# One written order with filling for the stages ahead of the experts, and inverse roots on VectorE

## The reference, cut to what matters

```python
mod = (s_c @ ada_w[l] + ada_b[l])            # 6 x 1024 columns: shift, scale, gate, twice
hx = rms_norm(x, norm1_g[l]) * (1.0 + sc1) + sh1
px = hx @ w_in                               # 2304 columns, split into groups A, B, C, D
ya = chunk_spatial_gating(aX, sgu_w, sgu_b)  # gelu, heads of v normed, a 128 x 128 product a head
yb = fourier_mix(bX)                         # two products with DFT matrices
yc = diff_attn_core(...)                     # group C: two softmaxes a head, their difference times v
yd = neighbourhood_attn_latent(...)          # group D: one softmax a head, with a window and a bias
y_lat = rms_norm(heads of [ya, yb, yc, yd], head_g) @ w_out
x = x + g1 * y_lat
aff = softmax((rms_norm(x, norm2_g[l]) * (1.0 + sc2) + sh2) @ router_w)   # 16 experts
gate, idx = top_k(aff.T, 32)                 # each expert takes 32 of 256 tokens
x = x + g2 * scatter(silu(xg @ wg) * (xg @ wu) @ wd * gate)
```

## Time and profile before

| | |
|---|---|
| median of 3 runs | 3203.36 us (3201.06 to 3207.66) |
| profiled execution | 3201.78 us, of it span 3200.0 us |
| TensorE / VectorE / ScalarE busy | 2916.9 / 908.9 / 550.2 us |
| mean granted TensorE clock | 0.946 |
| HBM read | 667 MB, 209 GB/s over the span |

### The profile page before, as it was taken

The page is one execution under the profiler, slowest core; times in us unless marked ns, Lnnn a source line. Parts: engine busy times, 40 slices in busy tenths (PEclk is TensorE's granted clock), DMA queues, the critical chain, the costliest instruction groups (busy, mean ns, idle before and its releaser), DMA issues.

```text
span 3200.0 us, 32009 instructions
## 1 busy us (share of the span) xinstructions
PE 2916.9 (91%) x12620; PEld 1682.0 (53%) x12620; DVE 908.9 (28%) x1838; ACT 550.2 (17%) x1059; POOL 91.3 (3%) x159
## 2 busy tenths in 40 slices
PE   6997689888889987999898999999999999999998
PEld 3554334333335544333333585665784686674883
DVE  2545431111114453101111343452100434343001
ACT  1243311111111241110110113230000113310000
POOL 3000000000001000000000100001000000000000
PEclk9997689999999987998988999999999999999999
DMA  9313129999996333999999542224434432224432
GB/s 283 127 49 125 53 88 410 410 410 410 410 405 198 119 138 132 374 409 410 410 410 407 169 154 71 92 74 139 157 116 167 151 131 79 85 74 161 154 130 81
DMA packets 237359, 669.76 MB, mean 209 GB/s; under 512 B 8064, under 2 KB 18616, under 8 KB 237248
## 3 DMA queue, kind: packets, MB, share of 16 engines
q1 hardware_dynamic: 230432, 653.28, 54.2%
q0 software_dynamic: 6816, 14.94, 2.0%
HBM read 667.09 MB, written 2.90 MB: 209 GB/s over the span
## 4 chain that ended last, share of the span: by engine, by line
PE 75%; DMA 17%; DVE 4%; issue 2%; ACT 1%; POOL 0%; SPq 0%; DVEq 0%; ACTq 0%; POOLq 0%
PE bank L768 31%; DMA ring<-in_exp_w_up_dram 16%; PE bank L781 9%; PE bank L1302 9%; PE bank L1320 5%; PE bank L1154 4%; PE bank L981 3%; PE bank L302 3%; PE bank L1177 1%; PE bank L921 1%; PE bank L1116 1%; PE bank L1032 1%; PE bank L822 1%; PE bank L943 1%; PE bank L1019 1%
## 5 line engine op out<-in xcount | busy, mean ns | idle before, releaser
L781 PE MATMUL bank<-ring,arena 128*64 128x512 f32 (+1 forms) x3072 | 711.0, 616 | 114.0 <-DMA ring<-in_exp_w_up_dram 64.7
L768 PE MATMUL bank<-arena,ring 128*128 128x256 f32 (+1 forms) x2496 | 530.2, 374 | 0.6 <-ACT arena L401 0.6
L781 PEld LDWEIGHTS bank<-ring,arena 128*64 128x64 f32 (+1 forms) x3072 | 217.8, 127 | 581.4 <-issue 470.9
L768 PEld LDWEIGHTS bank<-arena,ring 128*128 128x128 f32 x2496 | 463.9, 190 | 67.2 <-ACT arena L401 1.1
L768 PE MATMUL bank<-ring,arena 128*128 128x512 f32 (+1 forms) x1116 | 468.4, 580 | 3.2 <-DVE arena L2719 1.7
L768 PEld LDWEIGHTS bank<-ring,arena 128*128 128x128 f32 x1116 | 210.8, 190 | 250.4 <-issue 245.8
L1302 PE MATMUL bank<-ring,arena 128*128 128x512 f32 x640 | 297.2, 595 | 0.0
L302 PE MATMUL bank<-arena 128*128 128x128 f32 (+4 forms) x516 | 83.4, 310 | 116.3 <-DVE arena L2239 44.4
L1320 PEld LDWEIGHTS bank<-ring 128*128 128x128 f32 x1248 | 154.0, 192 | 42.0 <-issue 37.3
L2409 DVE COPY arena<-bank 128x512 f32<-128x512 f32 (+1 forms) x64 | 44.0, 688 | 452.0 <-PE bank L781 452.0
L1302 PEld LDWEIGHTS bank<-ring,arena 128*128 128x128 f32 x640 | 112.8, 192 | 93.8 <-issue 93.8
(11 more groups left out here) (293 smaller groups left out, 2156.2 us busy)
## 6 DMA issues: line engine op xcount, KB each, us to landing
ring<-in_exp_w_gate_dram SPq DMA_DIRECT2D x64, 2048.0 KB, 23.5
ring<-in_exp_w_up_dram SPq DMA_DIRECT2D x64, 2048.0 KB, 21.2
ring<-in_exp_w_down_dram SPq DMA_DIRECT2D x64, 2048.0 KB, 22.0
ring<-in_w_in_dram SPq DMA_DIRECT2D x42, 2048.0 KB, 7.7
ring<-in_ada_w_dram SPq DMA_DIRECT2D x24, 2048.0 KB, 11.7
ring<-in_w_ffn_up_dram SPq DMA_DIRECT2D x20, 2048.0 KB, 7.9
ring<-in_w_out_dram SPq DMA_DIRECT2D x8, 2048.0 KB, 9.9
ring<-in_w_ffn_down_dram SPq DMA_DIRECT2D x8, 2048.0 KB, 7.9
```

The source lines that it names most:

```text
L768: last = mm(o, lhs(k), rhs(k), start=start and k == 0, stop=stop and k == kt - 1)
L781: last = mm(U(us[c])[g * rows:(g + 1) * rows, :], lhs(k), rhs(i, c), start=(k < 2), stop=(k >= KT - 2))
```

## The change

Each stage becomes a generator of its own on each engine, with steps at the places where one engine waits for another: `ada(j)`, `late_a(t)`, `late_b(t)`, `fourier_of(s)`, `gate(t)`, `out_tile(t)` (21 steps), `gate_rows(g)`, `route(s)`, `gather(s)`. Every engine takes the steps in one written list, `PLAN`: J is a step of `attend`, a4 is a step of ada 4, o2 one of `out_tile(2)`, and so on. The slashes separate attention steps. Weights are fetched by name (`take`) and released at the next matmul that can do it (`let_go`). The loads A and B change places, and the slots are numbered anew.

The roots ahead of and in the first block move to VectorE: `inverse_roots` takes a first guess from the bits of the number and three Newton steps, 12 instructions, each waited for. ScalarE keeps the sums of squares; its Sqrt calls in this block go. The gating takes its roots for each tile instead of once for all. `out_tile` uses a free part of PROJ as room instead of `sgu_t`.

```diff
+SLOTS_2 = (2, 1, 0, 3)
+PRE_SLOTS = [(0, 1, 2, 3), (0, 2, 3, 1)]
+EXPERT_SLOTS = [(4, 5, 0, 2, 3, 1), (4, 5, 2, 1, 0, 3)]
+PRE_ORDER = "a0 a1 a2 a3 CQ DQ V a4 a5 A B a6 a7 a8 a9 w0 w1 a10 a11".split()
+PRE_PLACE = [(0, 1, 2, 3, 0, 1, 2, 3, 0, 1, 2, 3, 0, 2, 3, 0, 2, 3, 1),
+             (0, 1, 2, 3, 0, 1, 2, 3, 0, 1, 2, 3, 0, 1, 2, 3, 0, 1, 2)]
 PRE_CHUNKS = 19
+
+ATTENTION_PLAN = [
+    """a4 a4 / a4 / a5 a5 / a5 a4 / A0 A0 / a4 a5 A0 / a5 A0 / A0 r0 / A1 A1 g0 / A1 A1 g0 / A1 r0 g0 / r0 B0 B0 g1 /
+    B0 g0 g1 / g0 B1 B1 g1 / B1 g1 / g1 B2 B2 / B2 B3 B3 / B3 F0 F0 / F0 F1 / F1 / F1 F0 / F0 F0 / F1 F1 / F1 a6 a6 /
+    o0 a6 a7 a7 / o0 o0 a7 a6 / a6 a7 a8 a8 / a7 a8 a9 a9 / a9 a8 / a8 a9 / a9 o0 / o0 A2 A2 / A2 A2 o0 o0 / A2 o0 o0 /
+    o0 o0 / o0 o0 g2 / o0 A3 A3 g2 / o0 o0 A3 A3 g2 / A3 o0 / o0 g3 / o0 g2 g3 o1 / o0 o0 g2 g3 o1 o1 / g3 / g3 o1 / o1 /
+    o1 o1 / o1 o1 / o1 o1 / o1 o1 / o1 / o1 o1 / o1 / o1 / o1 / o1 o1 / R0 / R0 o2 / R0 o2 o2 / R0 o2 / o2 / o2 o2 /
+    o2 o2 / o2 o2 / o2 o2 / o2 / """,
+    """a4 a4 / a4 a5 a5 / a5 a4 A0 A0 / a4 a5 A0 A0 / a5 A0 r0 g0 A1 A1 / g0 A1 A1 / A1 r0 g0 g1 / r0 g1 B0 B0 /
+    B0 g0 g1 / g0 B1 B1 / B1 g1 / g1 F0 F0 / F0 / F0 F0 / F0 a6 a6 / a6 a7 a7 / a7 a6 / a6 a7 / a7 a8 a8 / a8 / a8 /
+    a8 o0 / o0 o0 / o0 / o0 / o0 o0 / o0 o0 / o0 o0 / o0 o0 / o0 a9 a9 / o0 o0 a9 / a9 / a9 / o0"""]
+TAIL_PLAN = [
+    """o3 G0 G0 o2 o2 o3 o3 G0 G0 o2 o2 o2 o3 o2 o2 o3 o3 o3 o3 o3 o3 o3 o3 o3 o3 G0 G0 o3 o3 G0 G0 o3 o3 G0 o3 o3 o3
+    R1 a10 a10 a10 R1 a11 a11 a11 a10 G0 R1 a10 a11 a11 r1 r1 r1 R1 G1 G1 G1 G1 G1 G1 G1 G1 G1 G1""",
+    """o1 o0 o0 o1 o1 a10 a10 o0 o0 a10 o1 o1 o1 o1 o1 o1 o1 o1 o1 o1 o1 a11 a11 o1 o1 a11 a10 o1 o1 a10 a11 a11 o1 o1 o1
+    r1 r1 r1 R0 R0 R0 R0 G0 G0 G0 G0 G0 G0 G0 G0 G0 G0"""]
+PLAN = [[name for part in a.split("/") for name in ["J"] + part.split()] + tail.split()
+        for a, tail in zip(ATTENTION_PLAN, TAIL_PLAN)]
 ALL = tuple(range(BANKS))
 DENSE, RULE, SIDE = (0, 1), (2, 3, 4, 5), (6, 7)
...
+        def follow(l, programs):
+
+            for name in PLAN[l]:
+                next(programs[name], None)
...
+            def inverse_roots(sums, n_terms, root, room):
+
+                step(ts(sums, sums, 1.0 / n_terms, EPS, ALU.mult, ALU.add))
+                step(ts(root.bitcast(I32), sums.bitcast(I32), 1, None, ALU.arith_shift_right))
+                step(ts(root.bitcast(I32), root.bitcast(I32), -1.0, 1597463007.0, ALU.mult, ALU.add))
+                for newton in range(3):
+                    step(stt(room, root, -0.5, sums, ALU.mult, ALU.mult))
+                    step(tt(room, room, root, ALU.mult))
+                    step(stt(root, room, 1.5, root, ALU.add, ALU.mult))
...
-        def ac_roots(src, n_terms):
-
-            return nc.scalar.activation(src, src, ACT.Sqrt, scale=1.0 / n_terms, bias=EPS)
-
         def ac_square_sums(nt):
 
             for t in range(nt):
-                nc.scalar.activation(XN[:, t, :], X[:, t, :], ACT.Square, accum_out=SST[:, t:t + 1]).then_inc(sem["scalar_step"], 1)
-                nc.scalar.wait_ge(sem["scalar_step"], ac.due("scalar_step"))
-            ac_roots(SST[:, 0:nt], D).then_inc(sem["root"], 1)
-            nc.scalar.wait_ge(sem["root"], ac.due("root"))
+                nc.scalar.activation(XN[:, t, :], X[:, t, :], ACT.Square, accum_out=SST[:, t:t + 1]).then_inc(sem["square_sum"], 1)
+                nc.scalar.wait_ge(sem["square_sum"], ac.due("square_sum"))
...
+                def take(name):
+
+                    s = PRE_SLOTS[l][PRE_PLACE[l][PRE_ORDER.index(name)]]
+                    nc.tensor.wait_ge(sem[f"chunk{s}"], pe.due(f"chunk{s}", 16))
+                    return slot[s]
+
+                def let_go(ins):
+
+                    if pending[0]:
+                        ins.then_inc(sem["chunk_used"], 1)
+                        pending[0] -= 1
+
...
+                def out_tile(t):
+
+                    yield
+                    yield
+                    yield
+                    turned = turned_xn(t)
+                    yield
+                    yield
+                    for c in range(2):
+                        if t == 0:
+                            weights[c] = take(f"w{c}")
+                        u = bank_for(DENSE)
+                        for k in range(KT):
+                            if c == 0 and k % 4 == 0:
+                                evacuated([turned[k // 4]])
+                            last = mm(U(u)[:, :], HT[:, k, t * P:(t + 1) * P], weights[c][:, k, :],
+                                      start=(k == 0), stop=(k == KT - 1))
+                            if k < KT - 1:
+                                let_go(last)
+                            else:
+                                last.then_inc(full[u % BANKS], 1)
+                                if t == tiles(l)[-1]:
+                                    pending[0] += 1
+                            if k % 2:
+                                yield
+                    yield
+                    yield
+                    yield
+                    turned = turned_xn(t)
+                    yield
...
+                def gate(t):
+
+                    nc.vector.wait_ge(free[a_units[t] % BANKS], dv.uses(a_units[t]))
+                    squares(PROJ[:, t, A_V:A_V + 256], HD, SS28[:, t, 0:4], PROJ[:, t, C_K:C_K + 256], "vector_step")
+                    yield
+                    yield
+                    inverse_roots(SS28[:, t, 0:4], HD, ROOT_GATE[t % 2], m["small"][:, 80:84])
+                    x = PROJ[:, t, A_V:A_V + 256].rearrange("p (g w) -> p g w", g=4)
+                    step(tt(x, x, bc(ROOT_GATE[t % 2], 2, [P, 4, HD]), ALU.mult), "vn_ready")
+                    yield
+                    u = dv.unit(lane=DENSE)
+                    yield
+                    landed(u)
+                    sv = PROJ[:, t, C_K:C_K + 256]
+                    frees(tt(sv.rearrange("p (h w) -> p h w", h=4), U(u)[:, 0:256].rearrange("p (h w) -> p h w", h=4),
+                             bc(COLS[:, 24:28], 2, [P, 4, HD]), ALU.add), u)
+                    step(tt(PROJ[:, t, 0:256], PROJ[:, t, 0:256], sv, ALU.mult))
+                    yield
...
+                    yield
+                    inverse_roots(SS[:, 16 * t:16 * t + 16], HD, ROOT_O[t % 2], m["small"][:, 60:76])
+                    yield
...
+                    yield
+                    yield
+                    nc.vector.wait_ge(sem["square_sum"], dv.due("square_sum"))
+                    inverse_roots(SST[:, t:t + 1], D, ROOT_X[:, t:t + 1], ROOM_X[:, t:t + 1])
+                    step(ts(XN[:, t, :], X[:, t, :], ROOT_X[:, t:t + 1], None, ALU.mult), "xn_ready")
```

More of the change, by code:

```diff
@@ L439, in qk_from @@
             return 0 if t in tiles(l) else 256
[L441 to L479, removed]
+        def follow(l, programs):
+            for name in PLAN[l]:
+                next(programs[name], None)
+            for name, program in programs.items():
+                assert next(program, "end") == "end", (l, name)
         @block.sync
@@ new lines, in late_b @@
+                def late_b(t):
+                    if t == 0:
+                        weights["B"] = take("B")
+                    w = weights["B"]
+                    u = b_units[t] = bank_for(DENSE)
+                    for k in range(KT):
+                        last = mm(U(u)[:, 0:256], HT[:, k, t * P:(t + 1) * P], w[:, k, 0:256], start=(k == 0), stop=(k == KT - 1))
+                        if k < KT - 1:
+                            let_go(last)
+                        else:
+                            last.then_inc(full[u % BANKS], 1)
+                            if t == tiles(l)[-1]:
+                                pending[0] += 1
+                        if k % 4 == 3:
+                            yield
+                    yield
@@ L971, in out_tile @@
                         last.then_inc(full[u % BANKS], 1)
[L972 removed]
+                        yield
                     yield
[L974 to L976 removed]
+                    evacuated(first)
+                    for t in range(2):
                         u = bank_for(DENSE)
[L978 to L989 removed]
@@ L1126, in gather @@
                         yield
-                filling = fill()
-                mix(attend(), filling, fill_table(l))
-                before_experts(l, filling, last_ada, route, gather)
+                programs = {"J": attend()}
+                for t in tiles(l):
+                    programs.update({f"A{t}": late_a(t), f"B{t}": late_b(t), f"g{t}": gate(t), f"o{t}": out_tile(t)})
+                for i in streams(l):
+                    programs.update({f"F{i}": fourier_of(i), f"R{i}": route(i), f"G{i}": gather(i)})
+                for j in range(4, 12):
+                    programs[f"a{j}"] = ada(j)
+                for i in range(2):
+                    programs[f"r{i}"] = gate_rows(i)
+                follow(l, programs)
+                assert pending[0] == 0 and held[0] == 1
```

608 lines of the change are left out of this document (281 added, 327 removed).

## The result

The changed kernel takes 3232.7 us (median of 4 runs, 3225.8 to 3236.7) against 3204.5 for the kernel before: a ratio of 1.0086, interval 1.0071 to 1.0102, so 28 us slower. I had said 3195 in 3172 to 3217. The profiled execution of the changed kernel took 3225.8 us for a span of 3223.8; before it was 3201.8 for 3200.0.

A forecast was written before the change was run, and what follows sets the result against it. Weights bound the expert stages; TensorE's waits on VectorE and its lower clock bound the stretches before them. Terms of 339 and 201.8 us gave a gain of 3, plus 5 for clock: 3203.4 - 8 = 3195 us, range 3172 to 3217.

The forecast's parts named there:

- parts 0 to 36: Layer 0, a part being one attention step and its fillers: TensorE 129 against VectorE 82, with additions 141 us.
- 7 at parts 24 to 27: Layer 0: 7 us added where ada folds queue behind the first out_tile's squares and roots.
- parts 0 to 16 and 29 to 33: Layer 1: the first run put at TensorE 62 plus 6.6 us, the second at 10.8 us.
- the stretches behind attention: From the end of attention to the first expert matmul: 85 us in layer 0, 75.2 in layer 1.
- Net 1.2 us longer for each of six tiles: Output tiles' chains: head roots 0.65 and token roots 1.85 us longer, less a table load of 1.28.
- The five microseconds taken as a share of the soft clock terms: Thin stretches of both layers: 5 of 24 us taken as gain in case TensorE's higher clock holds there.
- both stretches: First attention scores to first expert matmul: forecast 339 us in layer 0 and 201.8 in layer 1.
- Slower: Rival, chance 0.25: TensorE stands at fillers whose VectorE step comes behind another program's; 3216 us.
- seven places: Parts 13, 25, 37, 41, 57 and layer 1's 22, 30, where roots meet other work: 3 us each, 21 us.
- The filling works: Rival, chance 0.12: TensorE full except in four stretches and the routing, at the higher clock; gain 27, 3176 us.
- The two VectorE-bound stretches of layer 0: Parts 37 to 44 and 49 to 59, where VectorE's sum is larger: 33 and 40 us.
- the two thin spots: Layer 0, about 276 to 309 and 329 to 369: TensorE at clock 0.5 to 0.7, VectorE above 0.85 busy.

The follow-up runs named there:

- scalar_roots: The changed kernel in its written order, with the first block's roots made as before: Sqrt on ScalarE, then a reciprocal on VectorE; ratio 1.0015.
- one_step_roots: The changed kernel with each call of inverse_roots cut to one reciprocal, so its values are not the roots; ratio 0.9944.
- again_scalar: replanned_scalar with layer 0's order mended once more from part 30 on and three steps of layer 1 moved; ratio 0.9944.
- replanned_scalar: scalar_roots with its written order mended wherever a filler stood behind VectorE, in both layers, same steps; ratio 0.9968.

## Why the prediction was wrong

- **The step that failed: a queue priced by its sum.** In parts 0 to 36 of layer 0 I took TensorE as full, "TensorE 129, VectorE 82", because VectorE's sum is the smaller one, and priced what waits behind the roots there at "7 at parts 24 to 27": 141 us. It took 153.4. A sum does not see the order within a queue. Parts 24 to 31 cost 17 us above their work (8.4 waiting, 8.9 at the lower clock), 10 above my term; taking them apart gave back 11. The like in layer 1 makes parts 0 to 16 and 29 to 33 each 3 to 4 us too short, and the stretches behind attention are short by 3 to 5.
- **The same mistake in the price of the roots.** "Net 1.2 us longer for each of six tiles" makes 7 us. It prices a call as a latency on its tile's own chain, what it takes on VectorE against what ScalarE took, and leaves out who else waits in VectorE's queue. In the old order that was good enough (0 to 7 us); in the new one the move cost 23 (changed kernel against scalar_roots). This price is no term of the sum by parts; there the calls stand in VectorE's sums and are harmless wherever TensorE's sum is larger.
- **The five microseconds taken as a share of the soft clock terms** did not come; in layer 0 it went the other way. There the clock of the stretch fell from 0.84 to 0.81 and the busy time for the same matmuls rose from 278.7 to 288.9 us, while idle time rose only from 62.2 to 65.5. Ten of the 13.5 us lost in layer 0 are this. In layer 1 it is the reverse: busy time rose by 3.4 us (168.9 to 172.3), idle time by 8.5 (34.2 to 42.7). Over both layers the loss is about half clock and half waiting, in one execution of each kernel. The longest wait fell from 11.0 us to 7.45, but there are more of them, and the lower level stands behind short ones too. The four rows, before and changed for layer 0, then for layer 1 (the last one begins 0.54 us ahead of the first scores):

```profile
134.40:475.30 340.90, 278.65 (x1134) 157.83 (x1134) 160.75 (x418) 114.42 (x234) 9.60 (x19) 0.84 0.25 90
132.90:487.30 354.40, 288.87 (x1132) 165.15 (x1132) 182.73 (x553) 92.01 (x209) 9.60 (x19) 0.81 0.24 84
1081.70:1284.80 203.10, 168.90 (x712) 93.00 (x712) 91.74 (x227) 61.93 (x119) 3.30 (x6) 0.81 0.41 150
1094.00:1309.50 215.50, 172.31 (x712) 97.17 (x712) 103.20 (x294) 50.60 (x106) 3.29 (x6) 0.79 0.38 136
```

- **The sum.** The terms of both stretches were short by 15.4 and 13.2 us, and the 5 us did not come; the rest of the program took 1.6 less. That is 32.0 us, the distance from 3193.8 (3201.8 less the gain of 8) to the profiled 3225.8. The median lies 37.7 above the 3195; the other 5.7 us are in the main that the profiled execution is the fastest of the four, 6.9 below their median.
- **The rivals.** "Slower" had the right mechanism, a filler of TensorE behind roots in VectorE's queue, and two of its seven places: part 25, where the forecast's 7 and the rival's 3 make 10 us against 17 measured, and part 30 of layer 1, with a wait of 4.97 us against 3. At its places in parts 37, 41 and 57 nothing came above my terms. With 3216 it fell 17 us short. "The filling works", at 3176, was not reached by any kernel with the change's roots; one_step_roots, which leaves them out, came to 3184, with TensorE still at clock 0.80 from part 25 on.
- **Two loose readings** that moved nothing: the 60 us of the earlier trace rows are eight groups of waits and not eight waits, and the row of 691 ns that stands beside the section of the Trainium skill reads a bank, not SBUF.
- **What held.** The two VectorE-bound stretches of layer 0, to 1.1 us; a call at 2.3 us, and 2.53 on 16 columns where I had 2.6; the lower bound for integer operands; VectorE's busy time up by 45 us (I said 50); the longest wait 7.45 us, below 8; no table load in the attention of layer 0 but four for Gelu and four back; the routing of layer 1 bare for 8.4 us (6.6 and 1.8); both expert stages as long as before, to 3 us. Not so: attention ended at 397 instead of 389, the expert matmul came at 487 instead of 470, and besides the two thin spots (clock 0.67 and 0.54, VectorE busy 0.74 in each and not above 0.85) there was a third, at 219 to 262.

The Trainium skill, VectorE: DVE Perf Modes, section on the fixed extra latency of SBUF-source operations, asks for tiles of 512 columns and more. I had it beside the "slower" rival, at 0.25. These runs agree with it: a Newton instruction takes 160 ns on one column and 176 on sixteen, so nearly all of it does not depend on the width.

## What to carry to other kernels

When a chain of small instructions moves to an engine whose queue other work shares, price it twice: as latency on its own chain, and as delay of every copy queued behind it that another engine is waiting for. In an order written by hand, put each short copy or evacuation that a matmul waits for ahead of the long chain, even where that chain is the more urgent. Here a plan rewritten mainly by this rule was worth 28 us with the code otherwise unchanged. Sums by engine tell where an engine is the bound, but not that it is harmless elsewhere: list who stands behind whom there.

## What the runs showed of the hardware

- VectorE instructions on int32 cost the same as on float32, here in this small work (TENSOR_SCALAR on 16 columns: 177 ns on int32, 176 on float32). In the changed kernel (VectorE's groups by shape, 140 to 487; count, busy us, mean ns):

```profile
L2029 DVE SCALAR_TENSOR_TENSOR arena<-arena 128x16 f32<-128x16 f32 x12 | 2.1, 176 | 0.4
...
L2029 DVE SCALAR_TENSOR_TENSOR arena<-arena 128x1 f32<-128x1 f32 x12 | 1.9, 159 | 0.4
L2024 DVE TENSOR_SCALAR arena<-arena 128x16 int32<-128x16 int32 x4 | 0.7, 177 | 0.1
L2023 DVE TENSOR_SCALAR arena<-arena 128x16 f32<-128x16 f32 x4 | 0.7, 176 | 0.1
```

- Behind a wait of only 1.58 us (ahead of the fold at 224.92) TensorE ran at the lower level (1.2 GHz): the eight value products at 226.84 take 1.81 us instead of 1.00. The clock comes back and falls again (0.91 over 236.4 to 240, 0.67 over 240 to 250, 0.50 over 250 to 256) and stays at 1.00 only over the row from 262.2 to 286.4.
- The same wait is not always followed by the same level. TensorE in again_scalar, and under it in replanned_scalar, at the same place of layer 1:

```profile
1097.55 3.70 PE L993 MATMUL bank<-ring,arena 128*128 128x512 f32 x8 [1.80 <-ACT arena L1642]
```

```profile
1094.48 5.40 PE L993 MATMUL bank<-ring,arena 128*128 128x512 f32 x8 [1.80 <-ACT arena L1642]
```

Behind 1.80 us the eight products take 3.70 us in the one execution and 5.40 in the other. And the 17 executions of the kernel before that were taken beside the last three runs lie between 3198.6 and 3213.6 us. A difference of some 5 us between two single traces is therefore no finding here.
